# The second product of the feed-forward as seven half-size products (Strassen), its weight sums on GpSimd and its activation sums on VectorE

## The reference

```python
def sq_relu_mlp(h, w1, w2):
    a = jax.nn.relu(h @ w1)
    return (a * a) @ w2
...
h = layer_norm(DEEPNORM_ALPHA * h + sq_relu_mlp(h, mlp_w1[i], mlp_w2[i]), ln_g[i, 1], ln_b[i, 1])
```

## Time and profile before

| what | value |
|---|---|
| median of 3 runs | 1868.92 us (1868.83 to 1869.28) |
| the profiled execution: its own time | 1869.19 us |
| its span, first to last instruction | 1867.4 us |
| mean granted clock of PE | 0.999 |
| PE, DVE, ACT, POOL busy | 1849.6, 1139.3, 921.4, 184.2 us |
| DMA over the span | 162 MB, mean 87 GB/s |

### The profile page before, as it was taken

How to read it: one execution, slowest core, us unless ns; L and a number is a source line. 1 busy time by engine, 2 the same in 40 slices (tenths; PEclk the granted TensorE clock), 3 DMA queues, 4 the chain that set the end, 5 groups by cost and what they waited for, 6 DMA issues and landing times.

```text
span 1867.4 us, 26879 instructions
## 1 busy us (share of the span) xinstructions
PE 1849.6 (99%) x9640; PEld 1567.3 (84%) x9640; DVE 1139.3 (61%) x2007; ACT 921.4 (49%) x1825; POOL 184.2 (10%) x144
## 2 busy tenths in 40 slices
PE   9999999999999999999999999999999999999998
PEld 7888888878888888899999977888888889888987
DVE  6777676467443434657878877644444587456765
ACT  6665765353242424646767655423333365445551
POOL 0110101012000000400101024100000220011100
PEclk9999999999999999999999999999999999999999
DMA  6132113324322222313312123323222222330001
GB/s 202 46 113 68 46 67 138 113 74 166 115 97 90 90 90 90 91 46 93 90 45 68 46 95 131 113 98 115 102 90 90 90 102 82 123 108 1 1 0 45
DMA packets 118031, 162.01 MB, mean 87 GB/s; under 512 B 6576, under 2 KB 58544, under 8 KB 117936
## 3 DMA queue, kind: packets, MB, share of 16 engines
q1 hardware_dynamic: 116640, 156.04, 25.0%
q0 software_dynamic: 1296, 4.72, 0.8%
HBM read 158.64 MB, written 2.10 MB: 86 GB/s over the span
## 4 chain that ended last, share of the span: by engine, by line
PE 95%; DVE 2%; ACT 1%; DVEq 1%; SPq 1%; issue 0%; DMA 0%; ACTq 0%
PE psum L904 52%; PE psum L708 18%; PE psum L1078 8%; PE psum L673 4%; PE psum L1111 3%; PE psum L1345 2%; PE psum L859 1%; PE psum L937 1%; PE psum L998 1%; PE psum L866 1%; PE psum L854 1%; PE psum L1113 0%; PE psum L1250 0%; PE psum L1242 0%; PE psum L783 0%
## 5 line engine op out<-in xcount | busy, mean ns | idle before, releaser
L2445 DVE TENSOR_TENSOR w_lo<-slot,w_hi 128x512 fp32r<-128x512 f32 x302 | 232.3, 788 | 347.3 <-ACT w_hi L1663 347.1
L1663 ACT CAST w_hi<-slot 128x512 fp32r<-128x512 f32 x304 | 185.3, 622 | 426.1 <-PE psum L904 411.0
L904 PE MATMUL psum<-f_lo,w_hi 128*128 128x512 f32 x528 | 205.4, 389 | 0.0
L904 PE MATMUL psum<-f_hi,w_hi 128*128 128x512 f32 x512 | 199.8, 390 | 1.4 <-DVE f_lo L2493 1.0
L904 PE MATMUL psum<-w_hi,hid_hi 128*128 128x512 f32 x512 | 199.5, 390 | 0.0
L904 PE MATMUL psum<-w_hi,hid_lo 128*128 128x512 f32 x512 | 199.2, 389 | 0.0
L904 PE MATMUL psum<-w_lo,hid_hi 128*128 128x512 f32 x512 | 199.2, 389 | 0.0
L904 PE MATMUL psum<-f_hi,w_lo 128*128 128x512 f32 x512 | 199.2, 389 | 0.0
L3072 POOL TENSOR_TENSOR res<-rn,gb 128x1024 f32<-128x1024 f32 x16 | 46.3, 2891 | 827.5 <-DVE rn L2433 632.5
L904 PEld LDWEIGHTS psum<-f_lo,w_hi 128*128 128x128 f32 x528 | 99.1, 188 | 20.9 <-issue 0.2
L904 PEld LDWEIGHTS psum<-f_hi,w_hi 128*128 128x128 f32 x512 | 96.1, 188 | 22.7 <-DVE f_lo L2493 1.8
(11 more groups left out here) (396 smaller groups left out, 4368.2 us busy)
## 6 DMA issues: line engine op xcount, KB each, us to landing
slot<-in_w_mlp SPq DMA_DIRECT2D x128, 512.0 KB, 5.7
slot<-in_w_hgrn SPq DMA_DIRECT2D x32, 512.0 KB, 6.6
slot<-in_w_ssd SPq DMA_DIRECT2D x28, 512.0 KB, 5.6
slot<-in_w_ssd_out SPq DMA_DIRECT2D x16, 512.0 KB, 5.8
slot<-in_w_gate SPq DMA_DIRECT2D x16, 512.0 KB, 5.2
slot<-in_w_hgrn_out SPq DMA_DIRECT2D x8, 512.0 KB, 5.4
slot<-in_w_mla SPq DMA_DIRECT2D x8, 512.0 KB, 5.1
slot<-in_w_mla_out SPq DMA_DIRECT2D x8, 512.0 KB, 5.8
```

The costliest lines, as they stand in the source:

```text
L904: m = pe.matmul(psum[:, bank[c], cols or slice(0, width)], a, m_, start=opens and k == 0 and n_pass == 0, stop=closes and k == KD - 1 and ...
L1663: act.copy(w_hi[:, k, :], as_k(slot_of(stage, n))[:, k, :]).then_inc(high_made, 1)
L2445: dve.tensor_tensor(w_lo[:, k, :], as_k(slot_of(stage, n))[:, k, :], w_hi[:, k, :].bitcast(F32), ALU.subtract).then_inc(low_made, 1)
```

## The change

In the three loop quarters of each layer the second product, 512 tokens x 1024 hidden by 1024 hidden x 1024 columns, is cut in two halves each way: hidden tokens 0 to 255 and 256 to 511 (`a11`, `a12` and `a21`, `a22`, the second figure the half of the hidden columns), weights `b11`, `b12`, `b21`, `b22` in the two slots. Instead of eight half-size products there are seven, of sums of the halves, as Strassen and Winograd have it. Each product is 4 k rows x 2 token tiles x 3 passes.

- DVE makes four activation sums of 128x1024 (`a11 - a21`, `a21 + a22`, that minus `a11`, `a12` minus that) and the first weight sum `b12 - b11`, 4 instructions of 128x512. ACT and DVE split the four sums into high and low parts.
- POOL makes the other weight sums, 12 instructions of 128x512: `b22 - mixed`, `b22 - b12`, `b21 - mixed`. They lie in `res`, which is free in this stage, and in the slot.
- The rows of a product are split into half of `w_hi` and `w_lo` each, products in turn; a row is split once PE has begun the next row of the product two earlier.
- Results: 10 additions out of PSUM into `rn` by DVE, 2 copies out of PSUM by ACT, 4 additions into kept tiles (in `gb`) by DVE, and 6 additions of kept tiles to `rn` by POOL.
- The relus go straight into `fT` (eight tiles, no ring). The loads of the next `up` units wait until product 5, and product 6, is split. ACT waits for POOL's residual before the loop, POOL's load of the next gains stands behind the loop.
- The last quarter of each layer stays as it was.

The diff's core, indented less:

```diff
+PRODUCTS = 7
+PRODUCT_BANKS = (2, 0, 6, 4, 2, 0, 6)
+PRODUCT_CLOSES = (False, True, False, False, False, True, True)
+STEPS = 4 * PRODUCTS
...
+mixed = res[:].rearrange("p t d -> p (t d)").rearrange("p (a k n) -> p a k n", a=2, k=4)
+kept, kept_more = [gb[:, n, :].rearrange("p (t l) -> p t l", t=2) for n in range(2)]
...
+def product_operands(j, k):
+    return ((hid_hi[:, k, TOK[0]], hid_lo[:, k, TOK[0]]), (hid_hi[:, 4 + k, TOK[0]], hid_lo[:, 4 + k, TOK[0]]),
+            (hid_lo[:, k, TOK[0]], hid_rest[:, k, TOK[0]]), (hid_hi[:, k, TOK[1]], sum3_lo[:, k, :]),
+            (hid_lo[:, k, TOK[1]], hid_rest[:, k, TOK[1]]), (hid_hi[:, 4 + k, TOK[1]], hid_lo[:, 4 + k, TOK[1]]),
+            (hid_hi[:, k, TOK[0]], hid_rest[:, 4 + k, TOK[0]]))[j]
+def product_weights(j, k):
+    s0, s1 = as_k(slot_of("mlp0", 2)), as_k(slot_of("mlp0", 3))
+    return (s0[:, k, :], s0[:, 4 + k, :], mixed[:, 1, k, :], s1[:, k, :], mixed[:, 0, k, :], mixed[:, 1, k, :], s1[:, 4 + k, :])[j]
...
-    banks.stage(f"mlp{i}", [((kind, m), 4 * (u % 2) + m) for u, kind in enumerate(MLP_UNITS) for m in range(4)], QUARTERS)
+    banks.stage(f"mlp{i}", [((kind, m), 4 * u + m) for u, kind in enumerate(MLP_UNITS[:2]) for m in range(4)]
+                + [((j, t), PRODUCT_BANKS[j] + t) for j in range(PRODUCTS) for t in range(2)], QUARTERS - 1)
+    banks.stage(f"mlp_end{i}", [((kind, m), 4 * (u % 2) + m) for u, kind in enumerate(MLP_UNITS) for m in range(4)])
...
         def down(h, q):
-            load((P, KD, HALF), rows_cols(w_mlp2[i], q * D, h * HALF, HALF), f"mlp{i}", 2 + h, q, 4)
+            load((P, KD, HALF), rows_cols(w_mlp2[i], q * D, h * HALF, HALF), f"mlp{i}", 2 + h, q, 4,
+                 (low_made, (part0[f"mlp{i}"] + h + 1) * KD + q * (2 * KD)))
...
             down(0, q)
             down(1, q)
-            up(1, 0, q)
-            up(1, 1, q)
+            up(1, 0, q, (sig("product_low"), (steps + STEPS - 4) + q * STEPS))
+            up(1, 1, q, (sig("product_low"), (steps + STEPS) + q * STEPS))
...
+        def product(j, q):
+            quarter, sums = i * (QUARTERS - 1), {2: 2, 3: 1, 4: 3, 6: 4}
+            if j in sums:
+                pe.wait_ge(sig("sum_low"), (4 * quarter + sums[j]) + q * 4)
+            bank = {}
+            for k in range(4):
+                if j < 2:
+                    pe.wait_ge(sig("hidden_low"), (KF * i + 4 * j + k + 1) + q * KD)
+                pe.wait_ge(sig("product_low"), (STEPS * quarter + 4 * j + k + 1) + q * STEPS)
+                still = product_operands(j, k)
+                moving = [w[:, 4 * (j % 2) + k, :] for w in (w_hi, w_lo)]
+                for t in range(2):
+                    if k == 0:
+                        bank[t] = claim(stage, (j, t), q)
+                    rows = slice(t * P, (t + 1) * P)
+                    for n_pass, (a, m_) in enumerate(((still[0], moving[0]), (still[0], moving[1]), (still[1], moving[0]))):
+                        m = pe.matmul(psum[:, bank[t], :], a[:, rows], m_, start=k == 0 and n_pass == 0,
+                                      stop=k == 3 and n_pass == 2)
+                        if t == 0 and n_pass == 0:
+                            m.then_inc(sig("product_begun"), 1)
+                        if j < 2 and t == k == 0 and n_pass == 1:
+                            m.then_inc(units_begun, 1)
+                    if k == 3:
+                        m.then_inc(bank_full[bank[t]], 1)
...
-            for h in range(NHALF):
-                down(h, q)
+            for j in range(PRODUCTS):
+                product(j, q)
...
+        def product_high(j, k, q):
+            if j < 2 and (j, k) != (1, 3):
+                act.wait_ge(blocks_begun, (part0[stage] + 1) * KD + (4 * j + k + 2) + q * (2 * KD))
+            elif j < 2:
+                act.wait_ge(sig("product_begun"), (STEPS * quarters + 1) + q * STEPS)
+            else:
+                act.wait_ge(sig("product_begun"), (STEPS * quarters + 4 * (j - 2) + k + 2) + q * STEPS)
+            if j in (2, 3, 5):
+                act.wait_ge(sig("mixed"), (12 * quarters + 4 * {2: 0, 3: 1, 5: 2}[j] + k + 1) + q * 12)
+            if j == 4:
+                act.wait_ge(sig("first_mixed"), (4 * quarters + k + 1) + q * 4)
+            act.copy(w_hi[:, 4 * (j % 2) + k, :], product_weights(j, k)).then_inc(sig("product_high"), 1)
+        def sum_high(dst, src, n, q):
+            act.wait_ge(sig("sum_made"), (4 * quarters + n) + q * 4)
+            act.copy(dst, src).then_inc(sig("sum_high"), 1)
+        def quarter(q):
+            def relu(n, c):
+                b = full(stage, (MLP_UNITS[n], c), q)
+                act.activation(fT[:, 4 * n + c, :], psum[:, b, :], ACT.Relu).then_inc(bank_free[b], 1)
+            def high(n, c):
+                act.wait_ge(sig("squared"), (KF * i + 4 * n + c + 1) + q * KD)
+                tokens = slice(0, T) if n else TOK[0]
+                act.copy(hid_hi[:, 4 * n + c, tokens], fT[:, 4 * n + c, tokens]).then_inc(sig("hidden_high"), 1)
+            for c in range(3):
+                relu(0, c)
+            high(0, 0)
+            high(0, 1)
+            relu(0, 3)
+            high(0, 2)
+            high(0, 3)
+            sum_high(hid_hi[:, 0:4, TOK[1]], sum3, 1, q)
+            landed(act, stage, 2, q, 4)
+            for k in range(4):
+                product_high(0, k, q)
+            for k in range(3):
+                product_high(1, k, q)
+            for c in range(3):
+                relu(1, c)
+            high(1, 0)
+            high(1, 1)
+            relu(1, 3)
+            high(1, 2)
+            high(1, 3)
+            product_high(1, 3, q)
+            act.wait_ge(sig("product_begun"), (STEPS * quarters + 5) + q * STEPS)
+            sum_high(hid_lo[:, 0:4, TOK[0]], fT[:, 0:4, TOK[0]], 3, q)
+            for k in range(4):
+                product_high(2, k, q)
+            for t in range(2):
+                b = full(stage, (0, t), q)
+                act.copy(kept[:, t, :], psum[:, b, :]).then_inc(sig("first_kept"), 1)
+            for k in range(4):
+                product_high(3, k, q)
+            sum_high(hid_lo[:, 0:4, TOK[1]], fT[:, 0:4, TOK[1]], 2, q)
+            sum_high(hid_hi[:, 0:4, TOK[0]], fT[:, 4:8, TOK[0]], 4, q)
+            for j in range(4, PRODUCTS):
+                for k in range(4):
+                    product_high(j, k, q)
+            landed(act, stage, 4, q, 4)
+            for k in range(KD):
+                if k == 3:
+                    act.wait_ge(blocks_begun, ((part0[stage] + 2) * KD + 1) + q * (2 * KD))
+                else:
+                    act.wait_ge(sig("product_begun"),
+                                (STEPS * quarters + (24 + k if k < 4 else 16 + k) + 2) + q * STEPS)
+                act.copy(w_hi[:, k, :], as_k(slot_of(stage))[:, k, :]).then_inc(high_made, 1)
+            split_high(stage, 3, q, 2, unit=(5, q, 4))
...
+        act.wait_ge(res_ready, NT * (2 * i + 1))
...
+        def add_product(j, quadrants, q):
+            dve.drain()
+            if j == 0:
+                dve.wait_ge(sig("first_kept"), (2 * quarters + 2) + q * 2)
+                dve.wait_ge(sig("spread"), (6 * quarters + 1) + q * 6)
+            for t in range(2):
+                b = full(stage, (j, t), q)
+                for tokens, h in quadrants:
+                    rows = rn[:, 2 * tokens + t, h * HALF:(h + 1) * HALF]
+                    m = dve.tensor_tensor(rows, rows, psum[:, b, :], ALU.add)
+                m.then_inc(bank_free[b], 1)
+        def keep_sum(j, dst, q):
+            dve.drain()
+            for t in range(2):
+                b = full(stage, (j, t), q)
+                dve.tensor_tensor(dst[:, t, :], kept[:, t, :], psum[:, b, :], ALU.add).then_inc(bank_free[b], 1)
+        def product_low(j, q, ks=range(4)):
+            for k in ks:
+                dve.wait_ge(sig("product_high"), (STEPS * quarters + 4 * j + k + 1) + q * STEPS)
+                n = 4 * (j % 2) + k
+                dve.tensor_tensor(w_lo[:, n, :], product_weights(j, k), w_hi[:, n, :].bitcast(F32),
+                                  ALU.subtract).then_inc(sig("product_low"), 1)
+        def sum_low(dst, src, high, n, q):
+            dve.wait_ge(sig("sum_high"), (4 * quarters + n) + q * 4)
+            dve.tensor_tensor(dst, src, high.bitcast(F32), ALU.subtract).then_inc(sig("sum_low"), 1)
+        def quarter(q):
+            a11, a21, a12, a22 = [fT[:, 4 * n:4 * n + 4, tokens] for n in range(2) for tokens in TOK]
+            hidden(0, q)
+            dve.tensor_tensor(sum3, a11, a21, ALU.subtract).then_inc(sig("sum_made"), 1)
+            product_low(0, q)
+            sum_low(sum3_lo[:], sum3, hid_hi[:, 0:4, TOK[1]], 1, q)
+            product_low(1, q, range(3))
+            hidden(1, q)
+            product_low(1, q, range(3, 4))
+            dve.tensor_tensor(a21, a21, a22, ALU.add).then_inc(sig("sum_made"), 1)
+            landed(dve, stage, 3, q, 4)
```

(73 more changed lines are left out.)

57 lines of the change are left out of this document (38 added, 19 removed).

## The result

| | before | after |
|---|---|---|
| median | 1868.88 us (1868.83 to 1869.28, 4 runs) | 1945.56 us (1944.48 to 1946.17, 4 runs) |
| span of the profiled execution | 1867.4 us | 1944.0 us |
| mean granted clock of PE | 0.999 | 0.976 |

The ratio is 1.0409, with a 95% interval of 1.0391 to 1.0427: 76.7 us slower, 12.8 us for each of the six loop quarters. The forecast was 1935, 1900 to 1955.

What follows compares the result with a forecast made beforehand. TensorE, busy 99%, bounds the kernel while other engines stay ahead; with DVE and POOL taking turns, `up0` moves from 43.6 to 54.5, +10.9 us a quarter, x 6 = +65.6 on 1869.2: 1935 us, range 1900 to 1955.

Steps and rivals of the forecast that it cites:

- product 2 starts: Loop quarter: DVE's queue plus 5 POOL turns of 1.10 us put it at 19.0, where PE wants it at 10.9.
- product 4's first split: Loop quarter: after DVE's three additions out of PSUM and two low sums, at 38.2; PE waits another 5.8 us.
- `up0`: Next feed-forward unit after the seven products: starts at 54.5 us after `up1`'s end, where today it is 43.6.
- The price of a turn: DVE beside POOL: each 128x512 POOL subtraction costs DVE 1.10 us, lower bound 0, upper bound 1.27.
- from there PE has 3 products, 16.35 us: From product 4's start at 38.2, PE runs three products at full clock, 16.35 us, to `up0` at 54.5.
- the clock falls too: Rival: after each long PE stall 12 matmuls run at the lower clock, 2.7 us a quarter, 1951 us; chance 0.25.
- the prediction's own sign: Windows after PE's stalls: a lower clock and matmuls near 0.45 us apart would show the forecast wrong.
- its central case, turns without the clock: Loop quarters: DVE and POOL take turns, PE's clock holds, +10.9 us a quarter, 1935 us; chance 0.47.
- DVE keeps the ports: Rival: POOL gets in only at drains and DVE's waits for ACT, +6.7 us a quarter, 1909 us; chance 0.17.
- POOL costs DVE nothing: Rival: POOL's subtractions do not slow DVE, -0.2 us a quarter, 1868 us; chance 0.04.
- Plus copy and split 1.3: ready at 52.5: Load of `up0`'s weights after product 5's splits (43.9): 7.3 us plus 1.3, ready 2 us before PE wants it.
- Those named as hidden: Loop quarters: ACT's some 41 us of work in 98, `hidden(0)`, products 0's and 1's splits, ACT's residual wait cost nothing.

Runs made afterwards that it cites:

- The first experiment: Changed kernel with POOL's twelve weight subtractions a quarter cut to 8 of 512 columns, most of the weight sums left out: 1860.11 us, ratio 0.9954.
- filler: Changed kernel with PE multiplying during its waits, 32 matmuls before product 2 and 22 before product 4 in each loop quarter: 1935.58 us, ratio 1.0354.
- the runs at 1903.5 and 1934.3: Against the changed kernel: all twelve POOL weight subtractions moved to DVE, 1903.52 us; product 4's splits put before DVE's second addition, 1934.25 us.
- the fastest kernel: Changed kernel rebuilt: squares on ACT, three weight sums within `up1`'s time, earlier load, products 4 to 6 split before most additions: 1851.97 us, ratio 0.9907.

## Why the prediction was right, and where its number came short

Step by step, for the quarter shown (t = 0 is 562.15):

| step of the prediction | forecast t | measured t |
|---|---|---|
| low parts of the hidden values end | 4.8 | 4.8 (566.93) |
| product 2 starts | 19.0 | 18.65 (580.80) |
| PE's wait before it | 8.1 | 7.61 |
| product 3's last split | 30.9 | 30.4 (592.5) |
| product 4's first split | 38.2 | 37.8 (599.94) |
| PE's wait before it | 5.8 | 5.18 |
| product 5's last split | 43.9 | 43.4 (605.6) |
| `up0` | 54.5 | 56.2 (618.39) |

**The price of a turn.** 1.10 us was taken from two operations in the earlier trace rows, and 6.79 us for four splits, 0.60 + 1.10 each, is the same number. Everything up to product 4 stood within 0.5 us because of it (PE's wait before product 4 is shorter by 0.6, as PE itself ends product 3 later). The first experiment shows the cause: take most of POOL's work away and 85.5 us go. The Trainium skill, SBUF — State Buffer, on the engine side's contention, has whoever starts first hold the shared ports for one instruction; the trace of after agrees in the loops (the place of the earlier trace rows does not fit), from the first subtraction on, which found DVE between two operations: POOL ran its 1.29 us and DVE's sum beside it took 2.36 for 1.22.

```profile
569.36 2.36 DVE L2718 TENSOR_TENSOR fT<-fT 128x1024 f32<-128x1024 f32 x1
...
569.35 1.29 POOL L3300 TENSOR_TENSOR res<-slot,res 128x512 f32<-128x512 f32 x1 [45.39 <-DVE res L2716]
```

The Trainium skill, Perfetto Trace Analysis, Optimizing Scalar/DVE Operations, warns that moving work from DVE to GpSimd might not help since they share a port; here it was worse than that, 42 us dearer than DVE doing it alone (1945.56 against 1903.52).

**The clock.** The failed step is "from there PE has 3 products, 16.35 us". The rival *the clock falls too* was given 0.25 and priced at 2.7 us a quarter; it came, at 18.49 - 16.35 = 2.1 us here and 1.8 to 2.8 in the six. The filler's 16.64 says that 0.3 of this is not the clock's. From start to start (600.06 to 618.39) the three products take 2.0 more than 16.35, and with the other terms 0.3 us early, 54.5 + 2.0 - 0.3 = 56.2, as measured. Six times 1.9 is the 11 us between 65.6 and 76.7. By the prediction's own sign (a lower clock in the windows after the stalls) its central case, turns without the clock, is wrong; the time lies between that case and the rival, and inside the range because the range was drawn to hold both. The rival should have had the larger chance: no row before had a wait as long as those forecast, and the start in the earlier trace rows, the only evidence on what follows a long one, pointed to the lower level. That first price, 12 matmuls, was fair: 7, 9 or 12 followed each of the second waits. The rivals *DVE keeps the ports* and *POOL costs DVE nothing* are out for the loops, by the turns above.

**The load.** "Plus copy and split 1.3: ready at 52.5" left out 1.3 us between the end of the burst and ACT's first copy, and a turn with POOL's spread at the first split. In the changed kernel both were hidden, as PE came at 56.4; where stalls went, it became the bound that the prediction called next, in the runs at 1903.5 and 1934.3, and an earlier load took 6.7 us off the latter.

**Hidden costs.** Those named as hidden stayed so: PE waits for nothing before product 0 or 1, nothing before products 5 and 6 or `up0`, and nothing of ACT's wait for the residual reaches PE. DVE's additions into `rn` are twelve a quarter (72 in the trace), not the ten that the list of the change has; the two more stand behind product 6's splits, off the path.

## What to carry to other kernels

Before work is given to GpSimd "beside" VectorE, ask whether both read two operands from SBUF. In the loops here each GpSimd instruction cost VectorE 1.1 us for an operation VectorE does in 0.6, and the offload made the bottleneck worse. ScalarE took the squares in the fastest kernel while PE waited 0.4 us for hidden values in all; what that edit brought by itself was not measured. When a change shortens TensorE's work, count the neighbours' chains against the new due times, and price the clock behind each standstill as part of the standstill.
